# The moving tokens of the feature products in another order: 16 of the first half, 16 of the second, in turns

## The chip, the cores and the metric

The kernel runs on one core of one Trainium2 chip. The metric is the device time of one execution in microseconds (us), from the launch of the program to its end; smaller is better. TensorE multiplies a stationary operand (up to 128 x 128, loaded by a weight load) with a moving operand (up to 512 columns) and adds the result into PSUM. VectorE, ScalarE and GpSimd do the other arithmetic, and DMA queues bring the weights.

## The reference

Two small transformers, one behind the other, for one sequence of 256 tokens and a width of 1024, in float32:

```
x = first_block(x, mem, ...)     # an MLA layer and a sliding-window layer, each with
                                 # cross attention over 256 memory rows and a squared-ReLU MLP of 4096
x = rmsnorm(x)
x = second_block(x, c, ...)      # a layer of gated convolution and RG-LRU, then a layer of
                                 # stick-breaking attention; each with a SwiGLU of 2816, all modulated by c
```

Nearly all of the arithmetic is `tokens @ weights` with weights that are used once. Every such product runs over all 256 tokens.

## The kernel before

**Splitting.** A float32 weight block that has landed in `raw` is split into a rounded part `w_hi` and a rest `w_lo` (ScalarE L741 writes `w_hi`, VectorE L1256 writes `w_lo`), both of type float32r; the activations are split likewise, into `h_hi`/`h_lo` (the two halves of `h_both`), `a_hi`/`a_lo` (of `a_both`), `u_hi`/`u_lo`, `o_hi`/`o_lo` and `l_hi`/`l_lo`. One float32 product then is three float32r products, hi x hi, hi x lo and lo x hi. `product` (L2171) issues these three: L2173, L2174 and L2175.

**Two ways to multiply.** "By features" (`features`, L2177): the stationary operand is a 128 x 128 block of weights, and the moving one is a 128-feature chunk of the activations for all 256 tokens. The result, 128 output features by 256 tokens, is half a PSUM bank. "By rows" (`token_rows`): the activations are stationary and the weights move; this gives rows of tokens. `features` is called by `two_bank_slot` (the general weight block of 8 chunks by 512 columns: 2 banks x 2 blocks x 8 chunks), by the down projections of both MLPs (L2513) and of both SwiGLUs (L2694, 11 chunks by 256 columns), and by single blocks of `w_in` and `swa`. The first weight block of most phases goes through `as_chunks_arrive` or `shifted_slot`, which call `product` themselves, with the moving operand in its plain order.

**Where operands lie.** The weight ring has two slots of 16 KB each for `w_hi` and `w_lo`. Each row of a weight block of 128 columns begins at a multiple of 512 bytes from the start of `w_hi`. From the start of `w_hi` to the start of `h_both` the declarations put 32768 + 32768 + 8192 + 8192 + 192 bytes (`w_hi`, `w_lo`, `ada_raw`, `xT`, and a filler of 48 words, `line_h`), which is a multiple of 512 and 192 more. `a_both`, `o_hi`, `o_lo`, `l_hi` and each row of `h_both` lie at 192 bytes behind a multiple of 512, too. `l_lo` lies 64 bytes further, and the rows of `u_hi` and `u_lo` are 1152 bytes apart, so that each lies 128 bytes further than the one before. A row of `h_both` or `a_both` for one chunk has 256 words, 1024 bytes.

**Order.** TensorE's program is one list. `as_chunks_arrive` follows the normalisation, `two_bank_slot` the rest; between the two banks of every other slot of the first block and of `gate_up0`, `ada_reduce` puts four transposes (L2227). Consumers read whole PSUM blocks when `parts_done` says so.

Of the kernel before, what the change touches and what calls it, by code (L numbers as in the profile page):

```python
# [25 lines left out]
T = 256  # L26
# [142 lines left out]
def build(nc, a, out):  # L169
    ctx = ExitStack()  # L170
    with ctx:
# [153 lines left out]
        ps = ctx.enter_context(nc.psum_tensor("ps", [P, 8, BANK], F32))  # L325
# [65 lines left out]
        def ring(buf, slot, kc, cols):  # L391
            return buf[:, slot, 0:kc * cols].rearrange("p (c n) -> p c n", c=kc)
# [298 lines left out]
        def _(act):  # L691
# [51 lines left out]
            def squares_of_pair(name, q):  # L743

                src, squared, _, _ = norm_io(name)
                wait_pair(act, name, q)
                cut = slice(2 * q, 2 * q + 2)
                nc.scalar.activation(squared[:, cut, :], src[:, cut, :], ACT.Square).then_inc(norm_sq, 1)

            def shifted_high(name, q):  # L750

                hi, _, gains, shifts = shifted_io(name)
                wait_pair(act, "final" if name == "mix0" else name, q)
                if q == 0:
                    nc.scalar.activation(hi[:, :, T:T + 2], shifts.unsqueeze(2).to_broadcast([P, KD, 2]), ACT.Copy)
                for ch in (2 * q, 2 * q + 1):
                    ins = nc.scalar.activation(hi[:, ch, 0:T], xT[:, ch, :], ACT.Copy, scale=gains[:, ch:ch + 1])
                ins.then_inc(shifted_hi, 1)
# [93 lines left out]
            def squares_of(name):  # L852
                src, squared, _, _ = norm_io(name)
                nc.scalar.activation(squared[:, :, :], src[:, :, :], ACT.Square).then_inc(norm_sq, 1)
# [1315 lines left out]
        def _(pe):  # L2170
            def product(to, sh, sl, mh, ml, first, last):  # L2171

                nc.tensor.matmul(to, sh, mh, start=first, stop=False, skip_group_check=True)  # L2173
                nc.tensor.matmul(to, sh, ml, start=False, stop=False, skip_group_check=True)  # L2174
                return nc.tensor.matmul(to, sl, mh, start=False, stop=last, skip_group_check=True)  # L2175

            def features(s, b, blocks, hi, lo, first=True, last=True, chunk=0):  # L2177


                wh, wl = ring(w_hi, s.slot, s.kc, s.cols), ring(w_lo, s.slot, s.kc, s.cols)  # L2180
                for q, block_of in enumerate(blocks):
                    for c in range(s.kc):
                        ins = product(ps[:, b, q * T:(q + 1) * T], block_of(wh, c), block_of(wl, c),
                                      hi[:, chunk + c, :], lo[:, chunk + c, :],
                                      first and q == 0 and c == 0, last and q == len(blocks) - 1 and c == s.kc - 1)
                return ins

# [43 lines left out]
            def two_bank_slot(phase, j, i=None, step=0, reduce=None, hi=h_hi, lo=h_lo, apart=0):  # L2231


                s = Slot(phase, j, i, step)
                pe.wait_ge(split_lo, s.split + 2)
                for b in range(2):
                    if b and reduce is not None:
                        ada_reduce(reduce)
                    wait_acc(b, turn(phase, j, i, step) - apart)
                    features(s, b, [at_col((2 * b + q) * P) for q in range(2)], hi, lo).then_inc(parts_done, 1)  # L2240
# [101 lines left out]
            wh, wl = ring(w_hi, s.slot, s.kc, s.cols), ring(w_lo, s.slot, s.kc, s.cols)  # L2342
            for half in range(2):
# [3 lines left out]
                for q, col in enumerate((0, P + ROPE)):  # L2347
                    for c in range(4 * half, 4 * half + 4):
                        ins = product(ps[:, 0, q * T:(q + 1) * T], wh[:, c, col:col + P], wl[:, c, col:col + P], h_hi[:, c, :], h_lo[:, c, :],
                                      half == 0 and q == 0 and c == 0, half == 1 and q == 1 and c == KD - 1)  # L2350
# [8 lines left out]
            nc.tensor.transpose(ps[:, ADA_BANK, T:T + ROWS_B], rows_b[0:ROWS_B, :], ident[0:ROWS_B, 0:ROWS_B]).then_inc(vec_turned, 1)  # L2359
            wait_acc(1, t)  # L2360
            features(s, 1, [at_col(2 * P + ROPE)], h_hi, h_lo, last=False)
            wh, wl = ring(w_hi, s.slot, s.kc, s.cols), ring(w_lo, s.slot, s.kc, s.cols)
            for c in range(KD):
                ins = product(ps[0:ROPE, 1, T:2 * T], wh[:, c, P:P + ROPE], wl[:, c, P:P + ROPE], h_hi[:, c, :], h_lo[:, c, :],
                              False, c == KD - 1)
# [5 lines left out]
            for phase, name, hi, lo, n, banks in (("w_uq", "qn", cq_hi, cq_lo, 4 * QK, UQ_BANKS),  # L2371
# [4 lines left out]
                for g in range(3):  # L2376
# [5 lines left out]
                    if (phase, g) == ("w_uq", 0):  # L2382
                        for tile in range(NT):
                            ins = nc.tensor.transpose(ps[:, 7, tile * ROPE:(tile + 1) * ROPE], kropeT[:, tile * P:(tile + 1) * P],
                                                      ident[0:ROPE, 0:ROPE])
# [108 lines left out]
            def mlp(l):  # L2494
                as_chunks_arrive(f"up{l}", f"mlp{l}", banks=FIRST_UP_BANKS)
                ada_reduce(ADA_GROUP[f"w_o{l}"])
                two_bank_slot(f"up{l}", 1, apart=1)
                pe.wait_ge(all_summed, l + 1)
                nc.tensor.matmul(ps[:, NORM_BANK, 0:T], ones[:, :], scratch[:, 0, :], start=True, stop=True).then_inc(norm_total, 1)
                with pe.Fori(1, 4) as i:  # L2500
                    two_bank_slot(f"up{l}", 0, i, 2, reduce=i + (ADA_GROUP[f"up{l}"] - 1))
                    two_bank_slot(f"up{l}", 1, i, 2)
                for i in range(2):
                    for j in range(4):
                        s = Slot(f"down{l}", 4 * i + j)
                        pe.wait_ge(hid_lo, HIDDEN_BEFORE[str(l)] + 4 * (j + 1))
                        pe.wait_ge(split_lo, s.split + 2)
                        for b in range(2):
                            if (i, j, b) == (1, 0, 1):
                                wait_acc(0, turn(f"down{l}", i))  # L2510
                            if b == 1 and j % 2 == 0:
                                ada_reduce(ADA_GROUP[f"down{l}"] + 2 * i + j // 2 - 1)
                            features(s, DOWN_BANKS[i][b], [at_col((2 * b + q) * P) for q in range(2)], a_hi, a_lo,  # L2513
                                     first=j == 0, last=j == 3, chunk=KD * j).then_inc(parts_done, 1)
                ada_reduce(ADA_GROUP[f"down{l}"] + 3)
# [5 lines left out]
            for j in range(1, 4):  # L2521
# [7 lines left out]
                if j == 1:  # L2529
                    pe.wait_ge(r_ready, 1)  # L2530
                    for tile in range(NT):
                        ins = nc.tensor.transpose(ps[:, 3, tile * P:(tile + 1) * P], r_row[:, tile * P:(tile + 1) * P], ident[:, :])
# [85 lines left out]
            for g in range(2):  # L2618
                if g:
                    wait_acc(0, turn("lru_in", 2) + 1)  # L2620
                for c in range(4):
                    ins = nc.tensor.matmul(ps[:, RG_BANKS[g][c // 2], c % 2 * T:(c % 2 + 1) * T], rg_w[:, g, c, :], xr[:, c, :],
                                           start=c % 2 == 0, stop=c % 2 == 1, skip_group_check=True)
# [194 lines left out]
```

## Time and profile before

| | us |
|---|---|
| median of the runs shown | 1191.0 |
| the three runs | 1191.0, 1195.91, 1189.37 |
| span of the profiled execution | 1188.1 |
| TensorE busy in it | 1174.1 (99%) |
| VectorE, ScalarE busy in it | 864.7, 635.4 |

The span runs from the first to the last instruction of one profiled execution; its total time is not given apart from that. The span is 2.9 us below the median of the runs shown. A busy TensorE means that some matmul is under way. Matmuls overlap, so a matmul's own duration is longer than the step from one start to the next; the step is what counts for the time. The granted clock was 1.00 over the whole span.

### The profile page before, as it was taken

The page shows a single profiled execution, that of the slowest core. Times are in us where ns is not written, and L with a number is a line of the kernel's source. Part 1 is how long each engine was busy: PE and PEld are TensorE (multiplying, and loading weights), DVE is VectorE, ACT ScalarE, POOL GpSimd, SP SyncE. Part 2 cuts the span into 40 slices and gives each one's busy share as a digit, 9 for nine tenths or more (in the row PEclk, how much of TensorE's full clock was granted, in tenths as well). Part 3 has the DMA queues.
Part 4 walks back from the last instruction along what each step waited for, and adds up shares of the span by engine and source line. Part 5 has one row for each costly group of instructions (what it writes and reads, how often), then busy time and mean ns, then how long its engine had stood idle before and what let it go on. Part 6 is the DMA issues. An engine that isn't in the chain of part 4 may idle for free.

```text
span 1188.1 us, 23312 instructions
## 1 busy us (share of the span) xinstructions
PE 1174.1 (99%) x9605; PEld 1138.1 (96%) x9605; DVE 864.7 (73%) x1150; ACT 635.4 (53%) x853; POOL 95.6 (8%) x147
## 2 busy tenths in 40 slices
PE   8999999999999999999999999999999999999998
PEld 8999999999998999999999999999988879999998
DVE  5876898768776798777889988876567557855543
ACT  6558576633437567634368463443456575634332
POOL 0000011110125011111100001110000000000000
PEclk9999999999999999999999999999999999999999
DMA  9452587887772488788754557876645604565452
GB/s 316 147 178 72 191 305 256 305 293 247 264 266 72 159 288 297 264 286 301 269 201 143 167 173 252 294 271 200 207 169 182 211 1 142 173 207 187 146 195 84
DMA packets 150058, 248.95 MB, mean 210 GB/s; under 512 B 5553, under 2 KB 80922, under 8 KB 149978
## 3 DMA queue, kind: packets, MB, share of 16 engines
q1 hardware_dynamic: 135858, 197.17, 49.2%
q0 software_dynamic: 13952, 50.60, 11.8%
q8 instruction: 59, 0.97, 0.3%
q14 instruction: 21, 0.17, 0.0%
q10 hardware_dynamic: 168, 0.04, 0.0%
HBM read 246.74 MB, written 1.05 MB: 209 GB/s over the span
## 4 chain that ended last, share of the span: by engine, by line
PE 92%; DVE 1%; issue 1%; POOL 0%; ACT 0%; DVEq 0%
PE ps L2173 27%; PE ps L2175 27%; PE ps L2174 27%; PE ps L2453 2%; PE ps L2319 1%; PE ps L2764 1%; PE ps L2227 1%; PE ps L2435 1%; PE ps L2738 1%; PE ps L2422 1%; PE ps L2778 1%; DVE w_lo L1256 1%; PE ps L2254 0%; PE ps L2421 0%; PE ps L2765 0%
## 5 line engine op out<-in xcount | busy, mean ns | idle before, releaser
L1256 DVE TENSOR_TENSOR w_lo<-raw,w_hi 128x2048 fp32r<-128x2048 f32 (+4 forms) x196 | 412.7, 2144 | 101.8 <-ACT w_hi L741 101.5
L741 ACT ACTIVATE w_hi<-raw 128x2048 fp32r<-128x2048 f32 (+4 forms) x196 | 342.1, 1791 | 166.4 <-PE ps L2175 166.3
L2173 PE MATMUL ps<-h_both,w_hi 128*128 128x256 f32 (+1 forms) x1296 | 362.4, 280 | 1.4 <-issue 1.1
L2175 PE MATMUL ps<-h_both,w_lo 128*128 128x256 f32 (+1 forms) x1296 | 360.0, 278 | 0.0
L2174 PE MATMUL ps<-h_both,w_hi 128*128 128x256 f32 (+1 forms) x1296 | 360.0, 278 | 0.0
L2173 PEld LDWEIGHTS ps<-h_both,w_hi 128*128 128x128 f32 (+1 forms) x1296 | 242.7, 187 | 2.8 <-issue 1.9
L2174 PEld LDWEIGHTS ps<-h_both,w_hi 128*128 128x128 f32 (+1 forms) x1296 | 244.0, 188 | 0.1
L2175 PEld LDWEIGHTS ps<-h_both,w_lo 128*128 128x128 f32 (+1 forms) x1296 | 243.2, 188 | 0.0
L2173 PE MATMUL ps<-a_both,w_hi 128*128 128x256 f32 x864 | 240.9, 279 | 0.0
L2174 PE MATMUL ps<-a_both,w_hi 128*128 128x256 f32 x864 | 240.1, 278 | 0.0
L2175 PE MATMUL ps<-a_both,w_lo 128*128 128x256 f32 x864 | 240.1, 278 | 0.0
L2174 PEld LDWEIGHTS ps<-a_both,w_hi 128*128 128x128 f32 x864 | 163.5, 189 | 0.0
L2173 PEld LDWEIGHTS ps<-a_both,w_hi 128*128 128x128 f32 x864 | 162.2, 188 | 0.0
L2175 PEld LDWEIGHTS ps<-a_both,w_lo 128*128 128x128 f32 x864 | 162.2, 188 | 0.0
L1756 DVE SCALAR_TENSOR_TENSOR scratch<-ada_raw,silu_c,scratch 128x512 f32<-128x512 f32 x168 | 126.2, 751 | 9.1 <-DMA ada_raw<-in_l_ada_w 2.0
L567 POOL DMA_DIRECT2D ada_raw<-in_l_ada_w x96 | 69.5, 724 | 628.3 <-DVE scratch L1756 628.0
L1149 ACT ACTIVATE a_both<-a_full 128x512 fp32r<-128x512 f32 x18 | 11.4, 633 | 103.6 <-DVE a_full L2038 103.6
L1003 ACT ACTIVATE a_full<-ps 128x512 f32<-128x512 f32 x32 | 19.1, 597 | 52.8 <-PE ps L2175 52.1
L2173 PE MATMUL ps<-h_wide,w_hi 128*128 128x258 f32 x160 | 45.8, 286 | 0.0
L2174 PE MATMUL ps<-h_wide,w_hi 128*128 128x258 f32 x160 | 45.4, 284 | 0.0
L2175 PE MATMUL ps<-h_wide,w_lo 128*128 128x258 f32 x160 | 45.2, 283 | 0.0
L2173 PE MATMUL ps<-w_hi,h_both 128*128 128x512 f32 (+1 forms) x112 | 42.7, 381 | 0.7 <-issue 0.7
(421 smaller groups left out, 1816.3 us busy)
## 6 DMA issues: line engine op xcount, KB each, us to landing
ada_raw<-in_l_ada_w POOLq DMA_DIRECT2D x96, 512.0 KB, 6.6
raw<-in_mlp_w_up SPq DMA_DIRECT2D x32, 1024.0 KB, 6.3
raw<-in_mlp_w_down SPq DMA_DIRECT2D x32, 1024.0 KB, 6.3
raw<-in_l_ffn_w_gate SPq DMA_DIRECT2D x22, 1024.0 KB, 5.4
raw<-in_l_ffn_w_up SPq DMA_DIRECT2D x22, 1024.0 KB, 9.0
raw<-in_l_ffn_w_down SPq DMA_DIRECT2D x16, 768.0 KB, 5.7
raw<-in_l_w_qkv SPq DMA_DIRECT2D x12, 1024.0 KB, 6.5
raw<-in_l_w_in SPq DMA_DIRECT2D x10, 1024.0 KB, 6.6
```

Of the source, the lines that this page charges most:

```text
L567: pool.dma_start(ada_raw[:, slot, :, :], ada[l][:, 2 * quarter:2 * quarter + 2, group])\
L741: nc.scalar.activation(w_hi[:, s.slot, cut], raw[:, s.slot, cut], ACT.Copy).then_inc(split_hi, 1)
L1003: nc.scalar.activation(full, acc(b if j else FIRST_UP_BANKS[b]).rearrange("p (c t) -> p c t", c=2), ACT.Relu)\
L1256: nc.vector.tensor_tensor(w_lo[:, s.slot, cut], raw[:, s.slot, cut], w_hi[:, s.slot, cut].bitcast(F32), ALU.subtract).then_inc(split_lo, 1)
L1756: ins = nc.vector.scalar_tensor_tensor(ada_sum, w, c, ada_sum, ALU.mult, ALU.add)
L2173: nc.tensor.matmul(to, sh, mh, start=first, stop=False, skip_group_check=True)
L2174: nc.tensor.matmul(to, sh, ml, start=False, stop=False, skip_group_check=True)
L2175: return nc.tensor.matmul(to, sl, mh, start=False, stop=last, skip_group_check=True)
L2227: ins = nc.tensor.transpose(ps[:, ADA_BANK, q * P:(q + 1) * P], scratch[:, 2 + q // 2, (q % 2) * P:(q % 2 + 1) * P], ident[:, :])
L2319: ins = nc.tensor.transpose(ps[0:ncols, bank, ch * T + t * P:ch * T + (t + 1) * P], src(ch, t), ident[:, :])
L2422: nc.tensor.matmul(s[:, P:3 * P], q[:, P:T], k, start=False, stop=True, skip_group_check=True).then_inc(scores, 1)
L2453: ins = nc.tensor.matmul(ps[:, 6 + g % 2, qt * T + j * HD:qt * T + (j + 1) * HD], p[:, n * P:(n + 1) * P], v, start=j == 0 and n == 0, sto ...
```

## The change

`features` gives the moving operand and the PSUM destination another order of the 256 tokens: columns 0 to 15, 128 to 143, 16 to 31, 144 to 159, and so on. Each result still lands at its own token's place. The number of instructions, their operands, the bytes read and written and all waits stay. `as_chunks_arrive`, `shifted_slot` and `token_rows` are not touched.

```diff
+            def by_turns(tokens):
+
+                return tokens.rearrange("p (h j i) -> p j h i", h=2, i=16)
+
             def features(s, b, blocks, hi, lo, first=True, last=True, chunk=0):
 
 
                 wh, wl = ring(w_hi, s.slot, s.kc, s.cols), ring(w_lo, s.slot, s.kc, s.cols)
                 for q, block_of in enumerate(blocks):
                     for c in range(s.kc):
-                        ins = product(ps[:, b, q * T:(q + 1) * T], block_of(wh, c), block_of(wl, c),
-                                      hi[:, chunk + c, :], lo[:, chunk + c, :],
+                        ins = product(by_turns(ps[:, b, q * T:(q + 1) * T]), block_of(wh, c), block_of(wl, c),
+                                      by_turns(hi[:, chunk + c, :]), by_turns(lo[:, chunk + c, :]),
                                       first and q == 0 and c == 0, last and q == len(blocks) - 1 and c == s.kc - 1)
                 return ins
```

## Rows read from the trace of the kernel before

**Rows 1.** The page, busy time of each engine.

```profile
PE 1174.1 (99%) x9605; PEld 1138.1 (96%) x9605; DVE 864.7 (73%) x1150; ACT 635.4 (53%) x853; POOL 95.6 (8%) x147
```

**Rows 2.** The page, the chain that ended last, by engine and by line.

```profile
PE 92%; DVE 1%; issue 1%; POOL 0%; ACT 0%; DVEq 0%
PE ps L2173 27%; PE ps L2175 27%; PE ps L2174 27%; PE ps L2453 2%; PE ps L2319 1%; PE ps L2764 1%; PE ps L2227 1%; PE ps L2435 1%; PE ps L2738 1%; PE ps L2422 1%; PE ps L2778 1%; DVE w_lo L1256 1%; PE ps L2254 0%; PE ps L2421 0%; PE ps L2765 0%
```

**Rows 3.** Groups by line, products of the plain forms: operands, count, busy us, mean ns.

```profile
L2173 PE MATMUL ps<-h_both,w_hi 128*128 128x256 f32 (+1 forms) x1296 | 362.4, 280 | 1.4 <-issue 1.1
...
L2173 PE MATMUL ps<-a_both,w_hi 128*128 128x256 f32 x864 | 240.9, 279 | 0.0
```

**Rows 4.** Timeline of TensorE, 214 to 236 us: start us, us, instruction; 180 products apart.

```profile
214.49 0.28 PE L2174 MATMUL ps<-h_both,w_hi 128*128 128x256 f32 x1
...
235.69 0.28 PE L2174 MATMUL ps<-a_both,w_hi 128*128 128x256 f32 x1
```

**Rows 5.** Timeline of TensorE, 236 to 259 us; the last two lines 180 products apart.

```profile
236.28 0.60 PE L2227 MATMUL ps<-ident,scratch 128*128 128x128 f32 x4
236.63 0.37 PE L2173 MATMUL ps<-a_both,w_hi 128*128 128x256 f32 x1
236.84 0.29 PE L2174 MATMUL ps<-a_both,w_hi 128*128 128x256 f32 x1
...
237.89 0.28 PE L2174 MATMUL ps<-a_both,w_hi 128*128 128x256 f32 x1
...
258.29 0.28 PE L2174 MATMUL ps<-a_both,w_hi 128*128 128x256 f32 x1
```

**Rows 6.** L2174 in 213.9 to 236.1 us: ns min/median/max, first and last start.

```profile
L2174 PE MATMUL ps<-a_both,w_hi x16: 281/281/281, 230.7 to 236.0; 128*128 128x256 f32 x16
```

**Rows 7.** L2174 in 237.4 to 258.3 us, in the same form.

```profile
L2174 PE MATMUL ps<-a_both,w_hi x63: 276/276/279, 237.2 to 258.3; 128*128 128x256 f32 x63
```

**Rows 8.** Windows with L2174 at 281 ns: us, busy (count), clock, DMA.

```profile
168.60:190.80 22.20, 17.64 (x64) 12.07 (x63) 1.00 0.85 286
...
803.10:824.00 20.90, 16.63 (x60) 11.33 (x59) 1.00 0.64 212
sum 251.10, PE 199.60 PEld 136.16; mean PE 16.63 PEld 11.35
```

**Rows 9.** L2174 in 660 to 681 us (`lru_out`), in the form of Rows 6.

```profile
L2174 PE MATMUL ps<-l_lo,w_hi x61: 280/284/284, 659.7 to 680.9; 128*128 128x256 f32 x61
```

**Rows 10.** Groups of TensorE in 978 to 1166 us, plain and shifted forms.

```profile
L2174 PE MATMUL ps<-h_both,w_hi 128*128 128x256 f32 x351 | 96.9, 276 | 0.0
...
L2173 PE MATMUL ps<-u_hi,w_hi 128*128 128x258 f32 x64 | 18.3, 286 | 0.0
```

**Rows 11.** The chain in order of time: start us, us, what.

```profile
80.97 5.26 PE ps L2319 x48
```

**Rows 12.** All of line 2742: ns min/median/max, first and last start.

```profile
L2742 PEld LDWEIGHTS ps<-denied,far x16: 186/188/189, 941.2 to 970.2; 128*128 128x128 f32 x16
L2742 PE MATMUL ps<-denied,far x16: 278/334/386, 941.2 to 970.3; 128*128 128x256 f32 x16
```

**Rows 13.** Timeline of TensorE at 942.5 us.

```profile
942.48 0.51 PE L2742 MATMUL ps<-denied,far 128*128 128x256 f32 x2
942.82 0.40 PE L2173 MATMUL ps<-w_hi,h_both 128*128 128x512 f32 x1
```

**Rows 14.** Groups of VectorE by form: count, busy us, mean ns.

```profile
L2139 DVE TENSOR_SCALAR sb_l<-ps 128x384 f32<-128x384 f32 x16 | 8.2, 552 | 9.9 <-PE ps L2742 9.9
...
L1664 DVE TENSOR_TENSOR rope_tmp<-q_rows,cosT 128x384 f32<-128x384 f32 x2 | 1.1, 554 | 0.0
```

**Rows 15.** Windows over all engines: us, busy PE, PEld, DVE, ACT, POOL; clock, DMA.

```profile
237.40:258.30 20.90, 20.90 (x187) 20.90 (x186) 15.45 (x14) 7.45 (x4) 2.90 (x4) 1.00 0.86 302
```

## Prediction

> **What bounds the kernel now.** I read the page first. TensorE is busy for 1174.1 of 1188.1 us and VectorE for 73% [rows 1], and the chain that ended last is TensorE for 92%, with 81% in the three lines of `product` [rows 2]. So the time is the number of products times the step from one to the next. The clock is 1.00 (the 2.4 GHz level) in every window I asked for [rows 8, 15], so no part of the question is about the clock.
>
> The timeline gives the step. In a stretch around 237 to 258 us, 180 products take 258.29 - 237.89 = 20.40 us, 113.3 ns each [rows 5]; just before it, 180 products of the same shape take 235.69 - 214.49 = 21.20 us, 117.8 ns each [rows 4]. That is the first thing to see: the same work has two paces. Their mark in a list of groups is the mean duration, 281 ns in the slow one and 276 ns in the quick one [rows 6, 7]. The pace changes at an `ada_reduce`: four transposes, a product of 0.37 us, and the other pace holds until the next one [rows 5]. Twelve windows of the slow pace add up to 251.1 us [rows 8]; from 1025 us on, where no transposes stand between, all products run at 276 ns [rows 10].
>
> At the clock's 2.4 GHz, 256 columns would be 106.7 ns. The quick step is 6.6 ns above that, and the slow one 11.1 ns. What the extra depends on is the second thing to see: on where the moving operand lies against the weights. In `lru_out` the low part lies 64 bytes further than elsewhere against the weights, and its products take up to 284 ns [rows 9]. With `u_hi`, whose rows shift by 128 bytes from chunk to chunk, the mean is 286 ns, and two more columns (0.8 ns) don't make 10 ns of that [rows 10]. Both are in stretches where TensorE never waits. I read this as the two streams that TensorE reads from SBUF, moving columns and next weights, getting in each other's way at some distances between their addresses.
>
> **The change, part by part.** No instruction, wait, DMA or byte is added or removed. What changes is the order of addresses in `features`. Its products: `two_bank_slot` serves 36 weight blocks (1 of `w_o0`, 1 of `w_o1`, 7 + 7 of `up`, 1 of `lru_out`, 9 + 9 of `gate_up`, 1 of `sb_out`; the others of these phases go the two other ways) with 2 x 2 x 8 x 3 = 96 matmuls, 3456; the MLPs' down projections have 16 blocks of 96, 1536; the SwiGLUs' have 16 blocks of 2 x 11 x 3 = 66, 1056; `swa` and `w_in` have 192. Together 6240. The 864 x 3 with `a_both` [rows 3] are the second and third of these terms. At some 115 ns that is 0.72 ms, 60% of the span, and each nanosecond per product is 6.2 us.
>
> *A gain: the walks.* A weight block's row is 512 bytes and is read while the 1024 bytes of a moving row are, since each weight load hides under one product. Read in plain order, the moving address runs at twice the pace of the weight address. Taken modulo 512 bytes, the distance between them sweeps through every value once per product, the bad ones too. In turns, the moving stream reads 64 bytes at offset 64j and then 64 bytes at offset 512 + 64j: modulo 512 it advances as fast as the weights do. The distance stays near the 192 bytes that the declarations give, for the whole product. If interference is what separates the paces, the slow one goes: 251.1 us / 117.8 ns = 2130 products, times 4.5 ns = 9.6 us. A part of one of these windows belongs to `swa`'s first block and isn't touched (some 0.5 us), and `lru_out`'s second block (96 products, some 4 ns each, 0.4 us) comes in. I take 10 us. That modulo 512 is the right measure is my assumption; the rows only show that shifts of 64 and 128 bytes matter.
>
> *A further gain, bounded.* The lower bound for the step is that of weight loads alone: 48 transposes of 128 columns take 5.26 us, 109.6 ns each [rows 11]. If the extra of the quick pace is interference as well, 6240 x 3.7 ns = 23 us more. I don't take it: 113.3 ns holds to the tenth over long stretches, which looks like a fixed charge.
>
> *A cost, bounded.* Each product gets 15 jumps in the moving read and 15 in the PSUM write. The one product with a jump in both is L2742 (a broadcast read, two runs of 128 to PSUM). A pair of them at 942.48 ends 0.51 us later; with a duration of 278 ns for the second [rows 12] it starts at 942.71, and the next product at 942.82 [rows 13]. So its step is 0.11 us, to the hundredth that of a product with no jump, and a jump costs between nothing and some 5 ns. On VectorE, an operation over runs of 16 (L1664) takes 554 ns for 384 elements, and one over contiguous ones (L2139) 552 [rows 14]: jumps at such runs are free there. I take nothing. The upper bound is far off (15 x 5 ns x 6240 = 0.47 ms); one cycle of 0.42 ns per jump would be 15 x 0.42 x 6240 = 39 us, two would be 79 us.
>
> [...]
>
> *Cover.* A quicker TensorE asks for weights sooner. In the stretch at the quick pace VectorE has 15.45 of 20.90 us and DMA 0.86 [rows 15], and TensorE is busy throughout. DMA is the tighter of the two, but it kept up at 113.3 ns, and the gain that I take asks for no more than that pace. At 109.6 ns its share would be 0.89. If that cover failed, part of the further 23 us would become waits on `split_lo`.
>
> Sum: 0 for the instructions, 0 for the jumps, -10 for the pace. Against the profile that is a span of 1188.1 - 10 = 1178; the span is 2.9 us below the median of the runs shown, so 1191 - 10 = 1181.
>
> **The rivals.**
>
> *Jumps cost (slower).* Place: the address walk of the moving read, or of the PSUM write, at each of 15 run ends. For it: one jump at a step rounded to 10 ns can't exclude a cycle or two, and the quick pace has no slack (256 columns at one per cycle already fill 94% of it). Against it: rows 13 and 14. At one cycle per jump 1191 + 39 - 10 = 1220 with the gain and 1230 without; at two some 1260 to 1270. It decides from 0.11 ns per jump, where 15 x 6240 jumps eat the 10 us. Chance 0.22.
>
> *The slow pace becomes the rule (slower).* A distance that stays put is good only if it is a good one. If the two reads begin a part of a product apart, or the memory's period is another, the constant distance may be a bad one all along. Then the 6240 - 2130 = 4110 quick products get 4.5 ns each: 1191 + 18 = 1209. For it: whatever sets the pace is locked in by the phase after a transpose [rows 5], so phases do matter. Against it: the quick pace is found only where the offset is 192 bytes. Chance 0.13.
>
> *The order does not matter.* If the two paces come from how loads and products are issued, and not from addresses, they go on as now: 1191, within 2 us. For it: the pace flips at transposes, and both paces come with the same addresses. Against it: the longer durations with other offsets [rows 9, 10]. Chance 0.22.
>
> *The whole extra goes (faster by more).* 1191 - 10 - 23 = 1158. For it: this would be the first order in which the streams never meet. Against it: the constancy of 113.3 ns. Chance 0.10.
>
> **How the numbers follow.** The forecast has 0.33 and stands at 1181, its own range 1175 to 1187. About 0.5% (6 us) is what a measurement here can tell from no change. Of the forecast's 0.33, 0.03 lies within that, so that faster is 0.30 + 0.10 = 0.40, the same 0.22 + 0.03 = 0.25, and slower 0.22 + 0.13 = 0.35. The range for the time is 1165 to 1238: it takes in the forecast, no effect, the slow pace everywhere and one cycle per jump, and leaves out the whole extra (0.10) and dearer jumps (0.10).
>
> **What would show it.** In the changed kernel's profile: if the forecast holds, the products with `a_both` (all from `features`) have a mean of 276 ns instead of 279, the windows of 22.2 us between two `ada_reduce` shrink to some 21.4 us, and L2742, the transposes and the 258-column products stay. If jumps cost, every product of `features` is longer by the same amount, and the first blocks of each phase (plain order) are not: the two kinds differ side by side in the timeline. If the slow pace is the rule, the mean is 281 ns and the last 140 us of the span, now all at 276, grow by some 5 us. If the order does not matter, the windows of Rows 8 stand where they are. The prediction is wrong above all if a run of 16 is too short for TensorE's reads or writes at full rate, of which the trace of before has no case.

## The result and the profile after

The changed kernel is slower: 1221.05 us median of four runs (1220.45 to 1221.82), against 1190.18 for the kernel before (1189.34 to 1195.91). The ratio is 1.0244, 95% interval 1.0215 to 1.0273. The prediction of 1181 us was wrong in direction; the time lies inside the range to 1238.

First the page after: busy time of each engine and the chain by engine.

```profile
span 1218.5 us, 23312 instructions
PE 1206.2 (99%) x9605; PEld 1170.6 (96%) x9605; DVE 865.6 (71%) x1150; ACT 635.8 (52%) x853; POOL 95.4 (8%) x147
...
PE 92%; DVE 1%; issue 0%; POOL 0%; ACT 0%; DVEq 0%
```

The same instructions, the same chain, no new wait: TensorE is busy 32.1 us longer than in [rows 1], and the span is 30.4 us longer. The groups by line and form, and two starts of L2174 from TensorE's timeline, again 180 products apart:

```profile
L2173 PE MATMUL ps<-a_both,w_hi 128*128 128x256 f32 x864 | 245.5, 284 | 0.0
L2174 PE MATMUL ps<-a_both,w_hi 128*128 128x256 f32 x864 | 244.8, 283 | 0.0
```

```profile
240.89 0.28 PE L2174 MATMUL ps<-a_both,w_hi 128*128 128x256 f32 x1
...
262.49 0.28 PE L2174 MATMUL ps<-a_both,w_hi 128*128 128x256 f32 x1
```

21.60 us for 180 products are 120.0 ns each, where before there were 113.3 [rows 5] and 117.8 [rows 4]. The clock is still 1.00. In `features`, the two paces have become one. The last stretch shows it best, in which the kernel before had 276 ns throughout [rows 10]. L2174 of the changed kernel, in ns min/median/max, first in `sb_out`'s first block, which keeps the plain order, then in the turns of `gate_up1` and `ffn_down1` behind it:

```profile
L2174 PE MATMUL ps<-h_both,w_hi x32: 278/281/281, 998.4 to 1009.3; 128*128 128x256 f32 x32
```

```profile
L2174 PE MATMUL ps<-h_both,w_hi x277: 282/285/285, 1049.9 to 1149.3; 128*128 128x256 f32 x139
L2174 PE MATMUL ps<-a_both,w_hi x113: 282/282/285, 1149.6 to 1189.9; 128*128 128x256 f32 x113
```

The plain products are at the old slow pace (281 ns), and those in turns above it (medians 285 and 282 ns).

The sum comes out. 4110 products go from 113.3 to 120.0 ns (27.5 us) and 2130 from 117.8 to 120.0 (4.7 us): 32.2 us, against 32.1 more of TensorE's busy time and 30.4 of the span. A part of what was measured is not in the sum: the plain products of the last stretch went from 276 to 281 ns as well.

### The profile page after: what moved, and what is told of

The parts are those of the page before. It is cut to its first block, busy times and chain, and to the rows that moved or that the text cites. A ratio compares the mean times of both kernels' runs of the same rounds, so it can differ in the third digit from the quotient of the medians.

```text
span 1218.5 us, 23312 instructions
## 1 busy us (share of the span) xinstructions
PE 1206.2 (99%) x9605; PEld 1170.6 (96%) x9605; DVE 865.6 (71%) x1150; ACT 635.8 (52%) x853; POOL 95.4 (8%) x147
## 4 chain that ended last, share of the span: by engine, by line
PE 92%; DVE 1%; issue 0%; POOL 0%; ACT 0%; DVEq 0%
PE ps L2173 28%; PE ps L2174 27%; PE ps L2175 27%; PE ps L2457 2%; PE ps L2323 1%; PE ps L2768 1%; PE ps L2231 1%; PE ps L2439 1%; PE ps L2742 1%; PE ps L2426 1%; PE ps L2782 1%; DVE w_lo L1256 1%; PE ps L2258 0%; PE ps L2425 0%; PE ps L2769 0%
## 5 line engine op out<-in xcount | busy, mean ns | idle before, releaser
L2173 PE MATMUL ps<-h_both,w_hi 128*128 128x256 f32 (+1 forms) x1296 | 368.5, 284 | 0.7 <-DVE w_lo L1503 0.4
L2174 PE MATMUL ps<-h_both,w_hi 128*128 128x256 f32 (+1 forms) x1296 | 366.5, 283 | 0.0
L2175 PE MATMUL ps<-h_both,w_lo 128*128 128x256 f32 (+1 forms) x1296 | 365.9, 282 | 0.0
L2175 PEld LDWEIGHTS ps<-h_both,w_lo 128*128 128x128 f32 (+1 forms) x1296 | 246.0, 190 | 0.0
L2173 PE MATMUL ps<-a_both,w_hi 128*128 128x256 f32 x864 | 245.5, 284 | 0.0
L2174 PEld LDWEIGHTS ps<-h_both,w_hi 128*128 128x128 f32 (+1 forms) x1296 | 244.8, 189 | 0.1
L2174 PE MATMUL ps<-a_both,w_hi 128*128 128x256 f32 x864 | 244.8, 283 | 0.0
L2175 PE MATMUL ps<-a_both,w_lo 128*128 128x256 f32 x864 | 244.5, 283 | 0.0
L2174 PEld LDWEIGHTS ps<-a_both,w_hi 128*128 128x128 f32 x864 | 164.3, 190 | 0.0
L2174 PE MATMUL ps<-h_wide,w_hi 128*128 128x258 f32 x160 | 45.4, 284 | 0.0
```

## The experiments

Each has one run beside a run of the kernel before on the same chip, and a profile. "Step" is the mean time from one product's start to the next in the down projections (operand `a_both`), read from starts 180 apart or from the mark in the durations. One thing about these times has to be known first. The kernel before gave 1190.81, 1190.69, 1197.81, 1198.22 and 1190.26 us beside the five groups of runs, the second and third of them on one and the same chip. Its two paces are shared out anew in each execution (the first run shows it), so that a single time of plain order says nothing to within 8 us. Where a difference is smaller than that, the steps in the trace decide.

### Jumps or run ends, read or write

In `by_turns` (first run) and in `features` (second and third):

```diff
-                return tokens.rearrange("p (h j i) -> p j h i", h=2, i=16)
+                return tokens.rearrange("p (j i) -> p j i", i=16)
```

> All of features' operands, read and written, are described in runs of 16 that follow one another, so the addresses come in the plain order. Jump theory (the charge is for addresses that jump): steps of 113.3 and 117.8 ns as before, 1190 us. Run theory (the charge is for the end of every run of 16, wherever the next begins): 120 ns as in the changed kernel, 1221 us. Distance theory (a constant distance between moving and weight addresses is bad): as before, 1190 us.

It took 1195.7 us. The pattern was folded on the way to the instruction: the trace shows a plain run of 256 words, so this was the kernel before once more, and the question of run ends without a jump stays untried. It taught something else. Its L2174 from 1042 to 1166 us:

```profile
L2174 PE MATMUL ps<-h_both,w_hi x239: 281/281/281, 1041.9 to 1126.0; 128*128 128x256 f32 x120
L2174 PE MATMUL ps<-a_both,w_hi x113: 281/281/281, 1126.3 to 1165.9; 128*128 128x256 f32 x113
```

The whole last stretch ran at 281 ns, where the same instructions stood at 276 in [rows 10]. Some 1248 products at 4.5 ns are 5.6 us, as large as the difference of the two spans (1193.7 and 1188.1). So the pace is a state of the execution, not of the program: the instructions are the same in both.

```diff
-                        ins = product(by_turns(ps[:, b, q * T:(q + 1) * T]), block_of(wh, c), block_of(wl, c),
+                        ins = product(ps[:, b, q * T:(q + 1) * T], block_of(wh, c), block_of(wl, c),
```

> Only the moving operand is read in turns; results are written in plain order, so they land at the places of other tokens. If the charge is on the read side: step 120 ns and 1221 us. If it is the jumping PSUM write: 113.3 and 117.8 ns, 1190 us. The distance theory says 120 ns, since the distance of the reads is the changed kernel's.

```diff
-                                      by_turns(hi[:, chunk + c, :]), by_turns(lo[:, chunk + c, :]),
+                                      hi[:, chunk + c, :], lo[:, chunk + c, :],
```

> Only the results are written in turns, the moving operand is read in plain order; results land at the places of other tokens. The complement of the run before: write side 120 ns and 1221 us, read side or distance 113.3 and 117.8 ns, 1190 us.

Turns in the read alone: 1219.18 us. Turns in the write alone: 1195.91 us. One row of the groups of each, first the read, then the write:

```profile
L2174 PE MATMUL ps<-a_both,w_hi 128*128 128x256 f32 x864 | 244.8, 283 | 0.0
```

```profile
L2174 PE MATMUL ps<-a_both,w_hi 128*128 128x256 f32 x864 | 240.8, 279 | 0.0
```

The read has all of the charge: 283 ns is the changed kernel's mark and 120.0 ns its step. The write has none, and 15 jumps in PSUM at runs of 64 bytes are free here. The write-only kernel's time lies within what plain order does anyway, and the trace says it more sharply: all of L2174 is busy for 808.2 us, against 808.3 in the first run, which is plain in both.

### How the cost goes with the jumps

The same line of `by_turns` with other values:

```diff
-                return tokens.rearrange("p (h j i) -> p j h i", h=2, i=16)
+                return tokens.rearrange("p (h j i) -> p j h i", h=2, i=64)   # then i=32, i=8
+                return tokens.rearrange("p (j h i) -> p h j i", h=2, i=16)   # evens, then odds
+                return tokens.rearrange("p (h j i) -> p j h i", h=4, i=16)   # quarters in turns
```

> In turns of 64 tokens, results likewise: 3 jumps a product in place of 15. Jump theory: the extra of the changed kernel over the quick step, 6.7 ns, falls to a fifth, 1.3 ns, so some 115 ns and 1199 us or less. Distance theory: the distance modulo 512 bytes now sweeps half a turn and comes back, so that part of the interference stays: 116 to 119 ns, 1200 to 1215 us. A charge that does not depend on the number of jumps: 120 ns, 1221 us.

> In turns of 32 tokens, results likewise: 7 jumps a product. Jumps cost time only past the 3 that runs of 64 have for nothing. Jump theory with a price for each jump: between 113.3 and 116.4 ns for the quick step, 1191 to 1210 us. Distance theory: the distance of the reads modulo 512 bytes stays within 128 bytes of a constant, much as in the changed kernel, so about 120 ns, 1215 to 1221 us.

> In turns of 8 tokens, results likewise: 31 jumps a product, each back into the 64 bytes read just before by the turn after next. Jump theory: twice the changed kernel's extra, 113.3 + 13.8 = 127 ns, 1264 us. Distance theory: the walk modulo 512 bytes is the changed kernel's to within 32 bytes, 120 ns, 1221 us. If memory is read in 64-byte pieces and each piece is fetched anew at each run, far more than 127 ns: up to twice 113 ns.

> Runs of 16 and 15 jumps as in the changed kernel, but in the order: all even runs of a chunk, then all odd ones; results likewise. The moving address now runs at four times the pace of the weight address, and two neighbouring runs are 128 bytes apart, not 512. Jump theory: 120 ns, 1221 us. Distance theory: the sweep is back, so the slow pace at most: 113 to 118 ns, 1190 to 1205 us. Theory that two reads in a row 512 bytes apart (the same offset modulo 512) collide with each other: 113 to 118 ns too.

> Runs of 16 and 15 jumps, 16 tokens of each quarter in turns (256 bytes apart), results likewise. Jump theory: 120 ns, 1221 us. Distance theory: the moving address alternates between two offsets modulo 512, and moves on slowly at each: it meets the weights' offset for part of the product, so between 113 and 125 ns. Theory of collisions between reads 512 bytes apart: only every second neighbour but one is at the same offset, none are neighbours, so 113 to 118 ns, 1190 to 1205 us.

| order | jumps | time, us | step, ns |
|---|---|---|---|
| plain (before) | 0 | 1190.18 | 113.3 and 117.8 |
| turns of 64 | 3 | 1190.70 | 113.3 and 117.8 |
| turns of 32 | 7 | 1211.87 | 118.8 |
| turns of 16 (the change) | 15 | 1221.05 | 120.0 |
| quarters, 16 | 15 | 1220.19 | 119.9 |
| evens then odds, 16 | 15 | 1227.05 | 121.4 |
| turns of 8 | 31 | 1239.38 | 123.3 |

Starts of L2174, 180 products apart, of the turns of 64, then of the turns of 8, then of the evens and odds:

```profile
236.54 0.29 PE L2174 MATMUL ps<-a_both,w_hi 128*128 128x256 f32 x1
...
256.97 0.28 PE L2174 MATMUL ps<-a_both,w_hi 128*128 128x256 f32 x1
```

```profile
242.89 0.29 PE L2174 MATMUL ps<-a_both,w_hi 128*128 128x256 f32 x1
...
265.09 0.28 PE L2174 MATMUL ps<-a_both,w_hi 128*128 128x256 f32 x1
```

```profile
241.08 0.29 PE L2174 MATMUL ps<-a_both,w_hi 128*128 128x256 f32 x1
...
262.93 0.28 PE L2174 MATMUL ps<-a_both,w_hi 128*128 128x256 f32 x1
```

The turns of 64 take 20.43 us, against 20.40 [rows 5], and this stretch begins right behind an `ada_reduce`. Elsewhere in the same trace (215 to 230 us) L2174 has the slow pace's 281 ns, so this kernel has both paces, as before.

Two theories fall. Neighbours 512 bytes apart are not the cause: evens then odds has none, and is the dearest of the orders with 15 jumps. The prediction's walk modulo 512 bytes fails there too: that order brings the sweep back, which should have given 113 to 118 ns, and the step rises. More and shorter runs cost more, but there is no price per jump: 15 jumps cost 6.7 ns, 31 cost 10.0 and not 13.8, and 3 cost nothing.

### Where the streams lie

The filler in front of `h_both` is all that changes (16 and 64 words for the others); everything declared behind it moves with it, and the weights stay where they are:

```diff
-        sb("line_h", [P, 48])
```

> The changed kernel without the 48-word filler: moving operands and weights lie at the same offset modulo 512 bytes, where 192 bytes lay between them. Distance theory: the step changes clearly, by 3 ns or more per product in features (20 us or more), most likely up, since both streams walk modulo 512 at one pace and now at one place. Jump theory (short runs cost by themselves): features' step stays at 120.0 ns, 1221 us, and only the plain products change.

> The changed kernel with a filler of 64 bytes (16 words) for 192: distance 64 modulo 512. Distance theory: another step than at 0 and at 192, by 2 ns or more. Jump theory: 120.0 ns.

> The changed kernel with a filler of 256 bytes (64 words): distance 256 modulo 512, as far apart as it can be. Distance theory: the best of the places, under 117 ns and under 1203 us. Jump theory: 120.0 ns, 1221 us.

> The kernel before, plain order, without the filler: distance 0. Here every distance is swept once per product anyhow. If address distance sets the paces 113.3 and 117.8 ns, their share or size changes, by 1 ns or more in the mean (6 us or more); if the paces come from issue alone, 1190 us as before.

> The kernel before, plain order, with a filler of 256 bytes. If plain order is quick only where it meets the weights' address at the right moment, this place is between: mean step 113.3 to 120 ns, 1181 to 1221 us; if distance 0 alone is bad, 1190 us as at 192.

| distance modulo 512 bytes | turns of 16: us, step | plain: us, step |
|---|---|---|
| 0 | 1222.60, 120.0 ns | 1221.36, 120.0 ns |
| 64 | 1220.99, 120.0 ns | not tried |
| 192 | 1221.05, 120.0 ns | 1190.18, 113.3 and 117.8 ns |
| 256 | 1222.43, 120.0 ns | 1221.99, 120.0 ns |

Starts 180 products apart, in turns at distance 0, and in plain order at distance 0:

```profile
241.98 0.28 PE L2174 MATMUL ps<-a_both,w_hi 128*128 128x256 f32 x1
...
263.58 0.28 PE L2174 MATMUL ps<-a_both,w_hi 128*128 128x256 f32 x1
```

```profile
241.14 0.28 PE L2174 MATMUL ps<-a_both,w_hi 128*128 128x256 f32 x1
...
262.74 0.28 PE L2174 MATMUL ps<-a_both,w_hi 128*128 128x256 f32 x1
```

Plain order depends on the distance, by 31 us of the whole kernel. The turns do not at all: the distance that I wanted to hold fixed has no influence once it is fixed. Two limits of this table: since the weights never moved, it can't tell a distance between two streams from the place of the moving rows by itself, and plain order has three places only.

### Without most of the weight read

In the changed kernel, in the kernel before, and in the latter at distance 0, all chunks but the first of a block load 32 weight columns and not 128. What the other 96 output features of these products would add is left out.

```diff
+                        n = P if c == 0 else 32
-                        ins = product(ps[:, b, q * T:(q + 1) * T], block_of(wh, c), block_of(wl, c),
+                        ins = product(ps[0:n, b, q * T:(q + 1) * T], block_of(wh, c)[:, 0:n], block_of(wl, c)[:, 0:n],
```

> The changed kernel, in which all weight loads of features but those of each block's first chunk load 32 of the 128 columns; three quarters of these products are left out of the result. The moving side is the changed kernel's. Theory that the extra of the turns is made by the weight read beside it: the 32-column products step at 113.3 ns or little more, some 1190 us. Theory that the turns cost by themselves (jumps, short runs): 120 ns, 1221 us.

> The kernel before with the same 32-column weight loads; the same products are left out. If the slow pace of 117.8 ns is made by the weight read: it is gone, 113.3 ns throughout, some 1181 us. If it comes from issue: both paces stay, 1188 to 1192 us.

> Plain order, distance 0, 32-column weight loads; the same products are left out. With whole weight loads this place cost 120 ns. Weight-read theory: 113.3 ns or little more, some 1185 us. Otherwise 120 ns, 1221 us.

Turns 1220.71 us, plain 1180.31, plain at distance 0 1199.19. All of L2174 with `a_both`, weight loads and products, in ns min/median/max, for the turns, the plain order and the plain order at distance 0:

```profile
L2174 PEld LDWEIGHTS ps<-a_both,w_hi x864: 108/112/192, 234.3 to 1214.1; 128*32 128x32 f32 x154, 128*128 128x128 f32 x19
L2174 PE MATMUL ps<-a_both,w_hi x864: 280/283/287, 234.4 to 1214.2; 128*32 128x256 f32 x154, 128*128 128x256 f32 x19
```

```profile
L2174 PEld LDWEIGHTS ps<-a_both,w_hi x864: 107/108/192, 228.8 to 1173.7; 128*32 128x32 f32 x154, 128*128 128x128 f32 x19
L2174 PE MATMUL ps<-a_both,w_hi x864: 276/276/282, 228.9 to 1173.8; 128*32 128x256 f32 x154, 128*128 128x256 f32 x19
```

```profile
L2174 PE MATMUL ps<-a_both,w_hi x864: 276/280/283, 232.6 to 1192.7; 128*32 128x256 f32 x154, 128*128 128x256 f32 x19
```

This separates the two costs. The weight loads went from 188 to 108 ns, and the slow pace of plain order left with them: the median is 276 ns and the time 1180.31 us, 10 us below the median before, which is the size that I had given the slow pace. At distance 0 most of the charge left too (1221.36 to 1199.19 us), though not all: both paces are there again. TensorE's timeline of that run has all three within five microseconds. The first two lines stand 19 narrow products apart, the second and third three whole ones, the last two 15 narrow ones:

```profile
247.40 0.28 PE L2175 MATMUL ps<-a_both,w_lo 128*32 128x256 f32 x1
...
249.64 0.28 PE L2173 MATMUL ps<-a_both,w_hi 128*128 128x256 f32 x1
...
250.00 0.28 PE L2173 MATMUL ps<-a_both,w_hi 128*32 128x256 f32 x1
...
250.23 0.28 PE L2175 MATMUL ps<-a_both,w_lo 128*32 128x256 f32 x1
...
251.93 0.28 PE L2175 MATMUL ps<-a_both,w_lo 128*32 128x256 f32 x1
```

That is 117.9 ns, then 120.0 ns, then 113.3 ns a step. So the charge of 120.0 ns follows the whole weight loads even inside one execution, and a narrow load alone does not rule out the slow pace. The turns keep 283 ns. Their starts, 180 apart, are 21.60 us apart as in the changed kernel:

```profile
240.59 0.28 PE L2174 MATMUL ps<-a_both,w_hi 128*128 128x256 f32 x1
...
262.19 0.28 PE L2174 MATMUL ps<-a_both,w_hi 128*32 128x256 f32 x1
```

So the slow pace of plain order at 192 bytes and most of its cost at a bad distance need the whole weight load beside the moving read, and the cost of the turns does not: it is the moving read's own. A narrow load is narrower in three ways, though: it reads less, it takes less time, and the product writes 32 partitions of PSUM instead of 128. That it is the reading which matters fits the influence of the addresses, but no run separates the three.

Last, turns of 32 and of 8 with the same narrow loads:

> Turns of 32 tokens with the 32-column weight loads of e13; the same products are left out. Turns of 16 cost 6.7 ns by themselves there. If each run end costs the same, 8 of 16 ends cost half of that: 116.7 ns for the 32-column products, some 1200 us. If a stream that jumps often enough falls to another fixed pace: 113.3 or 120.0 ns, and what e5 had above or below that was the weight read.

> Turns of 8 tokens with the same weight loads. Each run end at one price: 32 ends, 126.7 ns, some 1262 us. Saturation of some kind: as e6 with whole weight loads, 123.3 ns, 1239 us.

1210.06 and 1239.16 us. Both stand within 2 us of their partners with whole loads (1211.87, 1239.38), and the starts of the second are 22.20 us apart again, 123.3 ns a product:

```profile
242.21 0.29 PE L2174 MATMUL ps<-a_both,w_hi 128*128 128x256 f32 x1
...
264.41 0.29 PE L2174 MATMUL ps<-a_both,w_hi 128*32 128x256 f32 x1
```

The curve over the number of jumps is therefore the moving read's own as well, and it flattens. One price per run end (116.7 and 126.7 ns expected) is refuted in both directions: the turns of 32 with narrow loads step at 118.3 ns, the turns of 8 at 123.3.

## Why the prediction was wrong

**What bounds the kernel, and the count.** Right. TensorE is the chain, nothing hides its products, and 6240 products times the change of their step gives the result within 2 us.

**The two paces as interference with the weight read.** Right in the main: with narrow loads the slow pace is gone and 10 us with it. It had only been argued; now it is shown that the width of the weight load decides at 192 bytes whether the slow pace occurs. That the step depends on addresses is shown too: the same plain order costs 113.3 and 117.8 ns at 192 bytes, and 120.0 at 0 and 256. The picture behind it was not right. If the distance really swept through every value once per product in plain order, the place where it starts should hardly matter, and it is worth 31 us.

**"A gain: the walks."** The two paces did vanish, and narrow loads make the turns no quicker, so beside the turns the weight read costs nothing that shows. Whether that is so because the streams no longer meet, as I had it, or because a slower moving stream hides the meeting, these runs don't tell. The assumption that the distance modulo 512 bytes decides is refuted for the turns: four distances, one step.

**"A cost, bounded": the failed step.** "I take nothing" for 15 jumps; they cost 6240 x 6.7 = 42 us over the quick pace. With the 10 us of the slow pace taken off and 42 put on, 1191 - 10 + 42 = 1223; measured 1221. The bound from L2742 (0 to 5 ns) was honest, the choice within it was not, and the reading behind the choice was off. It put the second product of the pair at 942.71 by the shortest duration of the 16. The timeline, asked for that product alone, has its start:

```profile
942.70 0.28 PE L2742 MATMUL ps<-denied,far 128*128 128x256 f32 x1
942.82 0.40 PE L2173 MATMUL ps<-w_hi,h_both 128*128 128x512 f32 x1
```

The step is 0.12 us and not 0.11, and it is 0.12 in the pair at 950.99 as well. That fits the slow pace without any charge, and it fits the quick pace with a charge of some 5 ns for one jump; it never spoke for zero. One jump, read to the hundredth of a microsecond, could not exclude 0.42 ns in any case, and the turns of 64 show why one jump is the wrong sample: three are free and fifteen are not. VectorE's runs of 16, 384 elements in 554 ns [rows 14], said nothing about a stream of 256 columns in 113.3 ns. The warning stood in the prediction itself: at 113.3 ns, 94% of the time is the columns' own, so the read has no slack. The rival "jumps cost" had place, size (1220 with the gain) and decision point right for this run length, at a chance of 0.22; its law, one cycle at each run end, is wrong (3 jumps would have cost 1.3 ns, and 31 would have cost 12.9).

**Write and read, against the pages.** The Trainium skill says in "PSUM — Partial Sum Buffer" (Specifications), and again in "Advanced Engine Details and Errata" (PSUM Cachelines), that any non-contiguous pattern slows matmuls significantly. The latter section adds that every two consecutive elements should be contiguous for best throughput, which runs of 16 satisfy. The write-only run fits the second statement and not the first: 1195.91 us, within the spread of plain order. The charge came from SBUF, where the Trainium skill, "Advanced Engine Details and Errata" (SBUF Cachelines), asks for at least two hits on each line of 16 bytes. Runs of 16 words give four, and even so the read was slower: by that rule nothing should have been lost, and the measurement decides.

**The other rivals.** "The slow pace becomes the rule" (1209) named a constant distance that is bad; the distance had no influence. "The order does not matter" and "the whole extra goes" fell with the first profile.

## What stays open

Why 3 jumps cost nothing, 7 cost 5.5 ns, 15 cost 6.7 and 31 only 10, and why evens then odds is dearer than turns with the same count. Run ends without a jump were not tried, since the pattern was folded. What decides which pace an execution takes after a stall is open as well. So is whether the distance between the moving rows and the weights counts or the place of the moving rows alone (the weights would have to be moved), and what of a narrow weight load does it. No order or filler tried is quicker than the kernel before.

## What to carry to other kernels

Where a float32r moving operand streams as fast as here, 256 columns in 113.3 ns, feed it in long contiguous runs: 64 words at a time cost nothing here, 32 or fewer cost 5 to 9% over the quick pace of 113.3 ns. The order in PSUM made no difference where it was tried, at runs of 16. When two readers of the same memory seem to interfere, try to shift one of them first; 192 bytes against 0 or 256 were worth 31 us of 1190. A bound taken from one event can't choose a price that is paid fifteen times; multiply its rounding by the count before choosing zero.

## What was unexpected of the hardware

Two executions of one program differ by up to 9 us of 1190 (1189.34 and 1198.22). The two traces of plain order at 192 bytes show what differs: whole stretches of matmuls run at 113.3 or at 117.8 ns each, at a granted clock of 1.00. Narrowing the weight loads from 128 to 32 columns removes the slower pace at 192 bytes, and at 0 bytes turns 120.0 ns into a mix of both paces. And three unrelated arrangements (turns of 16 at four distances, plain order at 0, plain order at 256) land on the same 120.0 ns to the tenth, 6.7 ns above the quick pace.
